# Bias rows in two early transfers, tables asked for by GpSimd, squares of x one modulation chunk earlier

## The reference

```python
def adaln_params(c, w, b, n):
    mod = jax.nn.silu(c) @ w + b
    return jnp.split(mod[:, None, :], n, axis=-1)

def trunk_layer(x, c, mixer, ...):
    sh1, sc1, gt1, sh2, sc2, gt2 = adaln_params(c, w_mod, b_mod, 6)
    y, new_state = mixer(modulate(rms_norm(x, g_mix), sh1, sc1))
    x = x + gt1 * y
    x = x + gt2 * moe_ffn(modulate(rms_norm(x, g_ffn), sh2, sc2), ...)
    return x, new_state
...
y = final_norm(x, c, w_mod_final, b_mod_final, g_final)   # two more modulation vectors
```

## Time and profile before

| what | value |
|---|---|
| median of 3 runs (lowest, highest) | 1871.53 us (1865.87, 1873.65) |
| the profiled execution, its own time | 1872.45 us |
| its span, first to last instruction | 1870.7 us |
| busy: PE, DVE, ACT, POOL | 1647.2, 1491.6, 1041.2, 217.4 us |
| mean granted TensorE clock | 0.90 of full speed |
| q1 (SyncE), q0 (GpSimd), q10 (ScalarE) moved | 460.45, 45.47, 21.42 MB |

### The profile page before, as it was taken

One profiled execution on the slowest core, in us unless ns is written; L12 is line 12 of the kernel. 1 busy time (PEld: TensorE's weight loads), 2 busy tenths in 40 slices (PEclk: granted clock), 3 DMA queues, 4 the chain that ended last, 5 costly groups with the idle time before them and its releaser, 6 DMA issues.

```text
span 1870.7 us, 23204 instructions
## 1 busy us (share of the span) xinstructions
PE 1647.2 (88%) x8604; PEld 1254.9 (67%) x8604; DVE 1491.6 (80%) x1629; ACT 1041.2 (56%) x1062; POOL 217.4 (12%) x278
## 2 busy tenths in 40 slices
PE   3998889789971699999999999999999999999950
PEld 2654754555541478888888888888888888888720
DVE  1379996333455599999999999999999999999938
ACT  2231116443321477777777777777777777777601
POOL 1024003000213110010010001001001001000031
PEclk7898998655985799999999999999999999999955
DMA  9235555000722499999999999999999999999672
GB/s 338 74 127 189 193 191 218 1 6 1 264 81 103 175 380 376 385 375 384 380 383 382 374 383 384 377 379 384 382 382 379 379 379 384 384 371 385 224 256 98
DMA packets 219287, 528.01 MB, mean 282 GB/s; under 512 B 9403, under 2 KB 14293, under 8 KB 219173
## 3 DMA queue, kind: packets, MB, share of 16 engines
q1 hardware_dynamic: 196000, 460.45, 67.1%
q0 software_dynamic: 13248, 45.47, 6.7%
q10 hardware_dynamic: 9988, 21.42, 3.0%
HBM read 493.88 MB, written 33.43 MB: 282 GB/s over the span
## 4 chain that ended last, share of the span: by engine, by line
PE 79%; DVE 7%; DMA 4%; ACT 3%; issue 3%; POOL 2%; ACTq 1%; SPq 0%; DVEq 0%; POOLq 0%
PE psum L1775 18%; PE psum L1777 18%; PE psum L1776 18%; PE psum L1605 5%; PE psum L1743 3%; PE psum L1709 2%; PE psum L1613 2%; PE psum L1724 2%; PE psum L1784 2%; PE psum L1764 2%; PE psum L1770 1%; POOL slot_dram L1500 1%; DMA front_ring<-in_w_in 1%; DVE final_work L1351 1%; PE psum L1717 1%
## 5 line engine op out<-in xcount | busy, mean ns | idle before, releaser
L1775 PE MATMUL psum<-split,turned 128*128 128x512 f32 x1536 | 611.2, 398 | 4.6 <-DVE turned L1276 4.6
L1777 PE MATMUL psum<-split,turned 128*128 128x512 f32 x1536 | 603.4, 393 | 0.0
L1261 DVE TENSOR_TENSOR low_late<-raw_late,split 128x2048 fp32r<-128x2048 f32 x192 | 430.9, 2285 | 37.8 <-ACT split L807 37.8
L1261 DVE TENSOR_TENSOR low_early<-raw_ring,split 128x2048 fp32r<-128x2048 f32 x194 | 443.5, 2287 | 19.1 <-ACT split L807 19.0
L807 ACT ACTIVATE split<-raw_ring 128x2048 fp32r<-128x2048 f32 x194 | 367.6, 1911 | 155.3 <-PE psum L1777 155.3
L807 ACT ACTIVATE split<-raw_late 128x2048 fp32r<-128x2048 f32 x192 | 356.7, 1909 | 38.0 <-PE psum L1777 38.0
L1775 PEld LDWEIGHTS psum<-split,turned 128*128 128x128 f32 x1536 | 289.8, 189 | 68.3 <-DVE low_late L1261 3.5
L1777 PEld LDWEIGHTS psum<-split,turned 128*128 128x128 f32 x1536 | 289.3, 188 | 66.4
L1776 PE MATMUL psum<-low_early,turned 128*128 128x512 f32 x768 | 302.4, 394 | 0.0
L1776 PE MATMUL psum<-low_late,turned 128*128 128x512 f32 x768 | 300.7, 392 | 0.0
L1519 POOL CAST bias_rows<-bias_raw 128x128 fp32r (+1 forms) x33 | 55.0, 1667 | 1026.6 <-PE psum L1777 1026.6
(11 more groups left out here) (328 smaller groups left out, 1787.1 us busy)
## 6 DMA issues: line engine op xcount, KB each, us to landing
raw_ring<-in_w_gate_up SPq DMA_DIRECT2D x97, 2048.0 KB, 10.5
raw_late<-in_w_down SPq DMA_DIRECT2D x64, 2048.0 KB, 10.6
raw_late<-in_w_gate_up SPq DMA_DIRECT2D x32, 2048.0 KB, 11.2
front_ring<-in_w_mod SPq DMA_DIRECT2D x12, 2048.0 KB
ys_dram<-expert_work ACTq DMA_DIRECT2D x33, 512.0 KB, 8.8
front_ring<-in_w_in SPq DMA_DIRECT2D x4, 2048.0 KB
front_ring<-in_w_mod_final SPq DMA_DIRECT2D x4, 2048.0 KB
ys_dram<-raw_ring POOLq DMA_DIRECT2D x1, 8192.0 KB, 28.3
```

The costliest lines, as they stand in the source:

```text
L1261: v.tensor_tensor(low(c)[:, half_of(x)], raw_slot(c)[:, half_of(x)], high(c)[:, half_of(x)].bitcast(F32), ALU.subtract).then_inc(low_made[ ...
L1775: mm(out, lhsT=x_hi, rhs=w_hi, start=start, stop=False)
L1777: return mm(out, lhsT=x_lo, rhs=w_hi, start=False, stop=stop)
```

## The change

Four things change together.

1. The biases of all sixteen modulation chunks come by two transfers that ScalarE asks for at the start: b_mod as 48 rows of 128 numbers and b_mod_final as 16 rows, into 64 partitions of one buffer. A bias product picks row 4t + q with a column of the identity matrix. SyncE's sixteen bias rows, GpSimd's clearing of three buffers and `pick2` are gone.
2. The seven transfers of tables and caches are asked for by GpSimd, when the chunk of `mod 3` has landed; w_gate and g_out come last.
3. The squares of x on ScalarE stand behind the copy of `mod 0`.
4. The scalings of x on VectorE stand behind the copy of `modT 0`.

```diff
-        bmod = [catA_flat[:, n * CW:(n + 1) * CW] for n in range(FRONT_RING)]
-        EARLY_MODS = 6
-        bmod2 = [cache_flat[:, n * CW:(n + 1) * CW] for n in range(FRONT_RING)]
+        bmod = pr.take(P)
...
-        parts = [2 if c[0] in ("mod", "kv") else 1 for c in chunks]
+        parts = [2 if c[0] == "kv" else 1 for c in chunks]
...
-                if c[0] == "mod":
-                    m = c[1]
-                    b = a["b_mod"][0, m * CW:(m + 1) * CW] if m < 12 else a["b_mod_final"][(m - 12) * CW:(m - 11) * CW]
-                    if m == 0:
-                        sp.wait_ge(bias_clear, 1)
-                    if m == EARLY_MODS:
-                        filled(sp, JOB[("cacheT", 7)])
-                    sp.dma_start((bmod if m < EARLY_MODS else bmod2)[s][0:1, :], b.unsqueeze(0)).then_inc(loaded[s], 16)
...
+            act_e.dma_start(bmod[0:48, :], a["b_mod"].rearrange("o (r n) -> (o r) n", n=P)).then_inc(bmod_in, 16)
+            act_e.dma_start(bmod[48:64, :], a["b_mod_final"].rearrange("(r n) -> r n", n=P)).then_inc(bmod_in, 16)
             for t in range(T):
                 act_e.dma_start(xs5[0:ROWS[t], t, :], x_rows(t)).then_inc(x_in, 16)
...
                 sc.activation(rr[:, 0:T], vv[:, 0:T], ACT.Sqrt).then_inc(x_sqrt, 1)
-                act_e.wait_ge(loaded[1], need[1])
-                act_e.dma_start(cs[:, 0:4, :], a["rope"][0:SEQ].rearrange("(t p) n -> p t n", p=P)).then_inc(tabs_in, 16)
...
-                    if t == 1:
+                    if t == 0:
                         x_squares()
...
-                    if t == 1:
+                    if t == 0:
                         x_scaled()
...
-            order(g.memset(pick2, 0.0))
-            order(g.memset(pick2[0:1, :], 1.0))
-            for x in bmod:
-                order(g.memset(x, 0.0))
-            note(pool, bias_clear)
...
+            pool.wait_ge(loaded[CH[("mod", 3)] % FRONT_RING], need[CH[("mod", 3)]])
+            pool.dma_start(cs[:, 0:4, :], a["rope"][0:SEQ].rearrange("(t p) n -> p t n", p=P)).then_inc(tabs_in, 16)
+            pool.dma_start(cs[0:DEC, 4, :], a["rope"][SEQ:NTOK]).then_inc(tabs_in, 16)
+            pool.dma_start(ckidx, a["cache_kidx"][0, 0].rearrange("(t p) n -> p t n", p=P)).then_inc(cache_in, 16)
+            pool.dma_start(ck, a["cache_k"][0, 0].rearrange("(t p) g n -> p t (g n)", p=P)).then_inc(cache_in, 16)
+            pool.dma_start(Vs[:, 0:8, :], a["cache_v"][0, 0].rearrange("(t p) g n -> p t (g n)", p=P)).then_inc(cache_in, 16)
+            pool.dma_start(wgate[0:16, :], a["gla_w_gate"][0]).then_inc(tabs_in, 16)
+            pool.dma_start(gout_b, a["gla_g_out"].to_broadcast([P, DV])).then_inc(tabs_in, 16)
...
-                        mm(bank(j)[32 * q:32 * q + 2, 0:P], lhsT=pick2, rhs=brow_[:, q * P:(q + 1) * P], start=True, stop=False)
+                        mm(bank(j)[32 * q:32 * q + 2, 0:P], lhsT=ident[0:64, 4 * t + q:4 * t + q + 1].to_broadcast([64, 2]),
+                           rhs=bmod[0:64, :], start=True, stop=False)
```

More of the change, by code:

```diff
@@ L222, in build @@
         idx_now = keep.take(1).bitcast(I32)
-        pick2 = keep.take(2)
         zero_i = keep.take(NBLK).bitcast(I32)
@@ L274, in build @@
         modrow = [pr.take(CW), pr.take(CW)]
-        cache_flat = pr.ap[:, pr.at - 2 * CW - 1536:pr.at - 2 * CW]
-        bmod = [catA_flat[:, n * CW:(n + 1) * CW] for n in range(FRONT_RING)]
-        EARLY_MODS = 6
-        bmod2 = [cache_flat[:, n * CW:(n + 1) * CW] for n in range(FRONT_RING)]
+        bmod = pr.take(P)
         twork = hi.take(PAST + DEC)
@@ L383, in build @@
         x_sq, x_var, x_sqrt, x_norm = sem("x_sq"), sem("x_var"), sem("x_sqrt"), sem("x_norm")
-        mod_copied, bias_clear = sem("mod_copied"), sem("bias_clear")
+        mod_copied, bmod_in = sem("mod_copied"), sem("bmod_in")
         mod_stored = [sem("mod_stored0"), sem("mod_stored1")]
@@ L1578, in _ @@
                     w = wslot(CH[s] % FRONT_RING)
-                    brow_ = (bmod if t < EARLY_MODS else bmod2)[CH[s] % FRONT_RING]
+                    if t == 0:
+                        pe.wait_ge(bmod_in, 32)
                     for q in range(4):
-                        mm(bank(j)[32 * q:32 * q + 2, 0:P], lhsT=pick2, rhs=brow_[:, q * P:(q + 1) * P], start=True, stop=False)
+                        mm(bank(j)[32 * q:32 * q + 2, 0:P], lhsT=ident[0:64, 4 * t + q:4 * t + q + 1].to_broadcast([64, 2]),
+                           rhs=bmod[0:64, :], start=True, stop=False)
                     for k in range(KD):
```

## The result

The changed kernel takes 1860.87 us (median of 9 runs, 1857.67 to 1866.16), before takes 1873.02 in the same rounds (9 runs, 1865.87 to 1877.35): ratio 0.9946, 95% interval 0.9926 to 0.9965. The forecast was 1860. Two more times the same kernel gave 1861.63 (ratio 0.9939) and 1863.46 (0.9958); the three ratios mean 0.9948, a gain of 9.8 us. The profiled execution of after, 1865.85 us, is one of its slowest, so the first profile shows less gain than the medians.

The account below looks back on a forecast made before the run. ScalarE's seven requests ahead of the copy of `mod 2` were taken to bound the first 50 us. Start -0.3, `mod 3` earlier -10.9 and clock -0.5 sum to -11.7 us from 1872.45: 1860.75, stated as 1860 us, range 1854 to 1868.

Parts of the forecast that it names:

- The bound: First 50 us: ScalarE's seven requests ahead of the copy of `mod 2` hold up `mod 3`; moving them and squares gives -10.9 us.
- Start (-0.3): Start of `mod 0`: no bias row behind the chunk to wait for; -0.3 us, ends 0 and -0.9.
- Squares: ScalarE behind `mod 0`: x lands at 17.7, squares begin at 18.6, `mod 1` copy 1.6 us late, `mod 3` at 33.55.
- Cover of chunk 3: Ahead of `mod 3`: chunk 3 lands at 30.6 us, leaving 3 us; beyond that each late microsecond costs one.
- Clock (-0.5): Products of `mod 3`: partly faster clock after less idling; -0.5 us, ends 0 and -1.6.
- Tables: Requests through GpSimd from about 31 us: tables land at about 52, VectorE needs them at 52.3; cost 0.
- The rest as fixed work: Behind the front: the gain is carried on, later chunks being asked for earlier by the same 11 to 12 us.
- B (x late): Rival in the front: x lands at 24.6 us, squares begin 6 us later, 1866.7 us; chance 0.10.
- C (GpSimd's queue one after another): Rival on the tables: seven serial transfers fill tabs_in at 95 us, TensorE stands still, 1895 us; chance 0.06.
- D: Rival behind the front: two thirds of the gain lost to weight waits or clock-dependent stretches, 1868 us; chance 0.12.
- The rule on VectorE and GpSimd's port: VectorE's scalings of x could delay GpSimd's table transfers by up to 3.39 us, to 55; sum unchanged.
- The signs: Right: no "issue" gap, `mod 3` at 33 to 34 us; wrong: squares wait for x, front under 9 us earlier.

Follow-up runs that it names:

- the bias part alone: Before with only the biases moved to two early transfers and the identity column: 1872.69 us, ratio 0.9999.
- the extra products: Changed kernel with identity-by-identity products ahead of TensorE's waits in the first 40 us: 1854.65 us, ratio 0.9910; again 1858.27 us, 0.9926.
- the tables alone: Before with only the seven requests moved to GpSimd, behind the chunk of `mod 3`: 1864.57 us, ratio 0.9956.
- squares alone: Before with only the squares and scalings of x moved behind the first modulation chunk, requests still on ScalarE: 1867.68 us, ratio 0.9981.

## Why the prediction was right, and where its sizes were off

**The bound.** It was the seven requests ahead of `mod 2`'s copy: taken away alone they give 8.75 us at `mod 3` and 8 us of the time; asked for by ScalarE, but behind the copies, they cost nothing that can be told; a gap named "issue" no longer stands ahead of a copy.

**Start (-0.3).** Undersized at its place, outside its own ends, and right in the sum: `mod 0` came 1.6 us earlier, `mod 1`, which waits for its chunk, only 0.3, and the bias part alone changed nothing that could be measured. I had written that GpSimd's clearing held up nothing but the first bias row; before, SyncE's request for chunk 1 stood behind that row too, and went out at 4.02 us. The chunk landed no later for it.

**Squares.** x landed at 18.0 instead of 17.7 us; the squares waited for it and yet began 0.6 us earlier than forecast, since the copy of `mod 0` was earlier too; the copy of `mod 1` stood at 25.49 (forecast 26.1), `mod 2` at 27.36 (27.95), `mod 3` at 33.43 (33.55).

**Cover of chunk 3.** I had it in at 30.6; GpSimd, which waits for it, went on at 32.80. Of the 3 us of cover some 0.6 were left. Nothing was lost by it, but with the extra products it is what `mod 3` waits for. The chunk did not come later than before: with the tables alone moved GpSimd went on at 32.92. My sum of bytes was short. It left out the next chunk, 1296 KB for `qi`, which SyncE asked for at 24.73 (24.47 before) and which shared the engines. From 0 to 32.8 us SyncE's queue moved this (columns as in the earlier trace rows):

```profile
q1 hardware_dynamic: 4798, 9.22, 78.8%
```

That is 0.83 MB more than the four chunks (8.39 MB), and 0.83 MB at the 383 GB/s of 19 to 33 us are 2.2 us.

**Clock (-0.5).** This term failed: it had the wrong sign. The products of `mod 3` took 3.60 us instead of 3.34, at half clock throughout, and `xT` behind them was slower too (10.37 instead of 9.46), which the sum had not considered. From `mod 3`'s start to the first rotary step it took 21.1 us instead of 19.6, +1.5 (19.7 in the second execution, +0.1). The Trainium skill's rule (TensorE: Matmul & The Clock Gate, "What's actually happening"), by which `mod 3` would have run at 2.4 GHz, did not decide here either: TensorE was busy 30 of the 38 us from 19 to 57 and had half its clock in two executions of three. With the idling filled, the level was up for most of the products, as the rule says.

**Tables.** Cost 0, right: VectorE's first rotary step waits for ScalarE's copy as before (3.58 us). The landing was mis-sized, on the safe side: the last table, asked for at 37.33, took 10.0 us and was in at 47.3 instead of 52, 7 us ahead of its use. Asked for by ScalarE, from 39.31 on, it landed at 53.4 and held VectorE 1.3 us.

**The rest as fixed work.** The lead at the first rotary step, 9.5, 10.9 and 9.4 us in the three executions, is 7.9, 10.6 and 8.0 at L1013, so most of it is kept. At the experts it is 5.8, 11.2 and 5.6. The router weights, for which VectorE waits in between, took 10.6, 7.3 and 10.3 us from request to landing (7.3 before): the lead shrank where they came late. That they are the cause is read from these three profiles and not tried. From the first expert product to the end it took 1243.5 us before and 1242.8, 1244.1 and 1244.7 in the three, so the experts' stretch did not change.

**Rivals.** B (x late) had the right place, but not the size: the squares wait for x by 1.44 us, of which 0.53 is the usual gap behind a copy. Its price, a microsecond of the time for each of x, was not shown: where x came 4.5 us late, chunk 1 came later still and decided. C (GpSimd's queue one after another) fell: the seven were in 14.5 us after the first request. D came true in part: from the first rotary step to the first expert product 3.7 of 9.5 us of lead were lost in the first execution, none in the second, 3.8 of 9.4 in the third. The rule on VectorE and GpSimd's port was not tested by the change, but it was touched by the tables alone: the scalings, beside GpSimd's requests, took 4.16 us instead of the 3.39 that they took before beside ScalarE's. The Trainium skill (SBUF — State Buffer, "SBUF: two separate sides") says that of VectorE and GpSimd the one that starts first gets their shared port for a whole instruction and the other waits. Here VectorE was the slower one; that the port did it is not shown.

**The signs.** Most came: no "issue" gap, the first square at 18.00, `mod 3` at 33.43, the wait ahead of the turn of `mod 2` at 1.45 us. But the first `qi` product came 9.5 us earlier (51.08 instead of 60.58), not 11.5, and two signs of being wrong came as well: the squares waited for x, and in two of three executions the front ended less than 9 us earlier (5.8 and 5.6).

The sum, -11.7, stands against -9.8 in the mean of three; in the executions at half clock the clock term alone (+1.5 instead of -0.5) is as large as the difference. That the first median, 1860.87, fell within 0.9 us of the forecast is in part luck: the same kernel gave up to 1863.46, and a chain that was right at `mod 3` (-10.98) was followed by losses that the sum did not have.

## What to carry to other kernels

A request for a transfer is work in its engine's order: put it where no copy stands behind it, on whichever engine that is, and not before the bytes that are needed first have landed. When a stall is taken away, ask what the clock does in the stretch that closes up, and price that from both sides; here filling TensorE's waits with spare products was worth another 4 to 7 us, by two measurements against the changed kernel's three. Judge a change of half a per cent by several executions, since one profile can be off by half of it.

## Hardware that I had not expected

- Two requests, each for 512 KB in pieces of 512 bytes, held ScalarE 2.64 and 4.03 us beside weight chunks (squares alone), and GpSimd 0.92 us each (after).
- The granted clock of one stretch of one kernel was 0.51, 0.82 and 0.51 in three executions, and a granted clock of 1.00 stood beside products that ran at the pace of 0.50 (3.59 us for 1.93).
- VectorE's scalings of 128x1024 took 904 ns in the median beside GpSimd's requests, 745 without.
- TensorE was at 0.54 of its clock in the attention while it was busy 80 of 95 us.
